# A two-block network: GpSimd's subtractions in eight operations a stage, and the written order of the steps replaced

## What is computed

```python
def first_block(x, ...):
    for l in range(DEPTH):                                   # DEPTH = 2
        proj = _rms(x, norm_g[l]) @ w_in[l]
        (gq, gk, gv, ga, gz, bq, bk, bv, iq, ik, iw, bz,
         cq, ck, cv, cz, gate) = jnp.split(proj, SPLIT_AT, axis=-1)
        y_a = _gla(gq, gk, gv, ga, ...) * silu(gz)           # linear attention with decay
        y_b = _dsa(bq, bk, bv, iq, ik, iw, ...) * silu(bz)   # an index picks 128 keys of each query
        y_c = _diff(cq, ck, cv, ...) * silu(cz)              # (softmax 1 - lam * softmax 2) V, 4 heads
        g = sigmoid(gate.reshape(B, T, 3, D_MODEL))
        x = x + (g[:, :, 0] * (y_a @ w_br[l, 0]) + g[:, :, 1] * (y_b @ w_br[l, 1])
                 + g[:, :, 2] * (y_c @ w_br[l, 2])) @ w_out[l]

def hybrid_layer(x, mod, ...):                               # second block, DEPTH layers
    h = rms_norm(x, norm1) * (1.0 + scale1) + shift1
    u, q, kv, gates = split(h @ w_in)
    mix = concatenate([pool_mixer(u), nsa_mixer(q, k, v, gates)]) @ w_out
    x = x + gate1 * mix
    h2 = rms_norm(x, norm2) * (1.0 + scale2) + shift2
    x = x + gate2 * (square(relu(h2 @ w_ff1)) @ w_ff2)       # 1024 to 4096 to 1024
```

## Time and profile before

| | |
|---|---|
| time before, median of 3 runs | 2624.44 us (2624.35 to 2630.99) |
| the profiled execution | 2632.11 us |
| its span, first to last instruction | 2630.3 us |
| TensorE busy, of the span | 2462.2 us, 94% |
| VectorE, ScalarE, GpSimd busy | 1337.0, 953.0 and 942.5 us |
| mean granted clock of TensorE | 0.975 |

### The profile page before, as it was taken

How to read it: one execution, slowest core, us unless ns; L and a number is a source line. 1 busy time by engine, 2 the same in 40 slices (tenths; PEclk the granted TensorE clock), 3 DMA queues, 4 the chain that set the end, 5 groups by cost and what they waited for, 6 DMA issues and landing times.

```text
span 2630.3 us, 34432 instructions
## 1 busy us (share of the span) xinstructions
PE 2462.2 (94%) x12303; PEld 1972.6 (75%) x12303; DVE 1337.0 (51%) x2835; ACT 953.0 (36%) x1691; POOL 942.5 (36%) x728
## 2 busy tenths in 40 slices
PE   7999989989999898998988898999998889899999
PEld 6687878678868686867887557888888656788887
DVE  4587243544368724354466545444566644522325
ACT  4442243432443224343244543322224444332221
POOL 4243414244434341423433103554544201344442
PEclk9999999999999999999999999999999989999999
DMA  5232414135423241413432102444433201233332
GB/s 174 72 97 90 151 35 142 50 103 177 135 71 96 87 161 33 137 49 112 171 99 61 33 3 71 160 161 150 163 118 99 69 1 33 65 97 96 96 96 81
DMA packets 132177, 256.04 MB, mean 97 GB/s; under 512 B 21915, under 2 KB 28589, under 8 KB 132013
## 3 DMA queue, kind: packets, MB, share of 16 engines
q1 hardware_dynamic: 132012, 253.83, 30.7%
HBM read 249.60 MB, written 4.19 MB: 96 GB/s over the span
## 4 chain that ended last, share of the span: by engine, by line
PE 79%; DVE 14%; ACT 4%; issue 2%; DMA 0%; DVEq 0%; SPq 0%; ACTq 0%
PE ps L818 65%; PE ps L772 4%; PE ps L1069 1%; PE ps L965 1%; PE ps L1118 1%; DVE arena L1768 1%; DVE top L1766 1%; PE ps L880 1%; PE ps L945 1%; ACT arena L1431 1%; PE ps L940 1%; DVE ps L1706 1%; DVE nsm L1477 1%; DVE ps L1704 1%; PE ps L1056 0%
## 5 line engine op out<-in xcount | busy, mean ns | idle before, releaser
L749 POOL TENSOR_TENSOR wl<-raw,wh 128x512 fp32r<-128x512 f32 (+2 forms) x724 | 942.3, 1326 | 1660.1 <-ACT wh L1139 1659.5
L818 PE MATMUL ps<-wh,hTh 128*128 128x512 f32 (+3 forms) x1600 | 633.6, 396 | 4.0 <-POOL wl L749 3.0
L818 PE MATMUL ps<-wh,hTl 128*128 128x512 f32 (+3 forms) x1600 | 614.7, 384 | 0.0
L818 PE MATMUL ps<-wl,hTh 128*128 128x512 f32 (+3 forms) x1600 | 614.5, 384 | 0.0
L1139 ACT ACTIVATE wh<-raw 128x1024 fp32r<-128x1024 f32 (+2 forms) x362 | 378.1, 1048 | 515.2 <-PE ps L818 269.9
L818 PEld LDWEIGHTS ps<-wh,hTh 128*128 128x128 f32 x1600 | 303.6, 190 | 77.8 <-issue 17.9
L818 PEld LDWEIGHTS ps<-wh,hTl 128*128 128x128 f32 x1600 | 303.1, 189 | 58.0
L818 PEld LDWEIGHTS ps<-wl,hTh 128*128 128x128 f32 x1600 | 304.0, 190 | 50.3
L818 PE MATMUL ps<-hTh,wh 128*128 128x512 f32 (+2 forms) x704 | 259.5, 369 | 5.6 <-DVE hTl L1710 2.3
L818 PE MATMUL ps<-hTl,wh 128*128 128x512 f32 (+2 forms) x704 | 258.2, 367 | 0.0
L818 PE MATMUL ps<-hTh,wl 128*128 128x512 f32 (+2 forms) x704 | 258.1, 367 | 0.0
(11 more groups left out here) (274 smaller groups left out, 3186.3 us busy)
## 6 DMA issues: line engine op xcount, KB each, us to landing
raw<-in_w_in_dram SPq DMA_DIRECT2D x160, 512.0 KB, 3.6
raw<-in_w_ff_dram SPq DMA_DIRECT2D x128, 512.0 KB, 3.6
modw<-in_w_mod_dram SPq DMA_DIRECT2D x96, 512.0 KB, 4.7
raw<-in_w_br_dram SPq DMA_DIRECT2D x24, 512.0 KB, 3.7
raw<-in_w_out_dram SPq DMA_DIRECT2D x24, 512.0 KB, 3.6
xm<-in_x_dram SPq DMA_DIRECT2D x8, 512.0 KB, 4.3
...
```

The source lines that it names most:

```text
L749: last = pool.tensor_tensor(low[part], whole[part], high[part], ALU.subtract)
L818: last = pe.matmul(*args, start=(q == 0 and c == 0 and n_pass == 0), stop=(q == u["quarters"] - 1 and c == u["chunks"] - 1 and n_pass == 2))
```

## The change

1. **GpSimd.** A stage's subtraction is made in eight operations in place of two: `128x128` each for a stage of 512 columns, 96 or 102 columns for the narrower ones. TensorE still waits for the last of a stage, where the semaphore is raised.
2. **The order.** `FIRST`, `SECOND` and `MOVED` are written anew. The work is the same but for the split of more sweeps in halves: the timeline has 2244 steps where it had 2222, with as many matmuls for each.
3. **A wait.** `rstd.bq` no longer stands between `small_turn` and the first `index` step, so the VectorE part of the first `index` step of a layer waits for ScalarE's part of `small_turn` itself.

That the roots of block two lie in the memory of the sums (PSUM) is so in both kernels; the code for it is not in the diff. The lines of the changed kernel that are named below stand 8 or 10 lower than before (749 is 757, 1893 is 1903).

The diff, with a few lines of each table:

```diff
@@ FIRST
-iq.0.0 q_turn.b.2 q_turn.b.3 iq.0.1 iq.0.2 iq.0.3 iq.1.0 iq.1.1 iq.1.2 iq.1.3 small.0.0 small_turn rstd.bq
+iq.0.0 q_turn.b.2 q_turn.b.3 iq.0.1 iq.0.2 iq.0.3 iq.1.0 rstd.bq iq.1.1 iq.1.2 iq.1.3 small.0.0 small_turn
...
@@ MOVED (of each engine's pairs those that the text speaks of)
-MOVED = {"act": """prob_turn.b.0.0>logit_exp.b.0.2 cq.1.1>prob_turn.b.1.1 decay3.2>decay3.3 mix0.0.2>mix0.0.1
+MOVED = {"act": """prob_turn.b.0.0>logit_exp.b.0.2 pair_exp.2.0.0>pool_band.1 pair_exp.1.1.2>pool_band.1 logit_exp.c.3.3>gate11.1.1
+                   k_rope.0>ek.1.2 pool.3>pair_turn.3.0.2 logit_exp.c.1.3>y_tok.c.0 ev.0.2>ev.0.1 bk.0.2>index.1.5
...
+                   prob.c.3.3>logit_max.c.3.3 prob.c.1.1>logit_max.c.1.1 y_tok.b.0>logit_max.b.2.0 evac.cz.1>logit_max.c.0.0
...
@@ -740,7 +748,7 @@
                 low, whole, high = piece(wl, g % RING, u), piece(raw, g % RING, u), piece(wh, g % SPLIT, u).bitcast(F32)
-                n = u["chunks"] * u["n"] // 2
+                n = u["chunks"] * u["n"] // 8
                 width = u["n"] if n >= u["n"] else n
@@ -1746,6 +1754,8 @@
                     W = WIDTH[t]
+                    if t == 0 and h == 0:
+                        dve.wait_ge(act_result, at("small_turned", l))
                     dve.wait_ge(act_result, at("relu", step))
```

More of the change, by code:

```diff
@@ L123 @@
-prob_turn.b.2.2 logits.b.3.1 logit_max.b.3.0 logit_exp.b.3.0 prob.b.2.3 value.b.2.0 prob_turn.b.2.3
-logit_exp.b.3.1 logits.b.3.2 logit_max.b.3.1 prob.b.3.0 value.b.2.1 logit_max.b.3.2 y_turn.b.1 ck.0.1
-prob_turn.b.3.0 logits.b.3.3 logit_exp.b.3.2 prob.b.3.1 value.b.2.2 ck.0.2 prob_turn.b.3.1 logit_max.b.3.3
-prob.b.3.2 logit_exp.b.3.3 value.b.2.3 y_tok.b.2 prob_turn.b.3.2 prob.b.3.3 value.b.3.0 ck.0.3 prob_turn.b.3.3
-value.b.3.1 y_turn.b.2 ck.1.0 value.b.3.2 value.b.3.3 rstd.cq y_tok.b.3 ck.1.1 ck.1.2 y_turn.b.3 ck.1.3 rstd.ck
@@ new lines @@
+prob_turn.b.0.2 value.b.0.0 logits.b.1.0 logits.b.1.1 logit_max.b.1.0 logit_exp.b.1.0 prob.b.0.3 cq.0.3
+logits.b.1.2 prob_turn.b.0.3 cq.1.0 logit_max.b.1.1 logit_exp.b.1.1 prob.b.1.0 value.b.0.1 prob_turn.b.1.0
+logits.b.1.3 logit_max.b.1.2 prob.b.1.1 q_turn.c.0 value.b.0.2 logit_exp.b.1.2 q_turn.c.1 prob_turn.b.1.1
+logits.b.2.0 logit_max.b.1.3 logit_max.b.2.0 value.b.0.3 prob.b.1.2 logit_exp.b.1.3 y_tok.b.0 cq.1.1
+prob_turn.b.1.2 logits.b.2.1 logit_exp.b.2.0 prob.b.1.3 value.b.1.0 prob_turn.b.1.3 logits.b.2.2 logit_max.b.2.1
@@ new lines @@
+logit_exp.b.2.1 prob.b.2.0 y_turn.b.0 cq.1.2 logit_max.b.2.2 prob_turn.b.2.0 logits.b.2.3 value.b.1.1
+logit_exp.b.2.2 prob.b.2.1 value.b.1.2 cq.1.3 prob_turn.b.2.1 logits.b.3.0 logit_max.b.2.3 logit_exp.b.2.3
+prob.b.2.2 value.b.1.3 y_tok.b.1 ck.0.0 q_turn.c.2 q_turn.c.3 logits.b.3.1 logit_max.b.3.0 logit_exp.b.3.0
+prob.b.2.3 prob_turn.b.2.2 value.b.2.0 prob_turn.b.2.3 logit_exp.b.3.1 logits.b.3.2 logit_max.b.3.1 value.b.2.1
+y_turn.b.1 ck.0.1 prob.b.3.0 logit_max.b.3.2 logits.b.3.3 prob.b.3.1 prob_turn.b.3.0 prob.b.3.2 value.b.2.2
@@ new lines @@
+logit_exp.b.3.2 ck.0.2 logit_max.b.3.3 prob_turn.b.3.1 logit_exp.b.3.3 value.b.2.3 prob_turn.b.3.2 prob.b.3.3
+ck.0.3 prob_turn.b.3.3 value.b.3.0 value.b.3.1 y_turn.b.2 ck.1.0 value.b.3.2 value.b.3.3 y_tok.b.2 rstd.cq
+y_tok.b.3 ck.1.1 ck.1.2 y_turn.b.3 ck.1.3 rstd.ck cv.0.0/ cv.0.0 cv.0.1 cv.0.2 cv.0.3 key_turn.ck.0
+key_turn.ck.1 cv.1.0 key_turn.ck.2 cv.1.1 cv.1.2 cv.1.3 cz.0.0 cz.0.1/ cz.0.1 cz.0.2 cz.0.3 cz.1.0 cz.1.1 cz.1.2
+key_turn.ck.3 cz.1.3 gate10.0.0 logits.c.0.0 logit_max.c.0.0 logit_exp.c.0.0 gate10.0.1 logit_max.c.0.1
@@ new lines @@
+prob.c.1.2 logit_max.c.1.3 logit_exp.c.1.3 value.c.0.3 y_tok.c.0 br10.0.1 prob_turn.c.1.2 logits.c.2.0
+logit_max.c.2.0 value.c.1.0 logit_exp.c.2.0 br10.1.0 prob_turn.c.1.3 prob.c.1.3 prob.c.2.0 logits.c.2.1
+logit_max.c.2.1 logit_exp.c.2.1 value.c.1.1 br10.1.1 prob_turn.c.2.0 logits.c.2.2 prob.c.2.1 logit_exp.c.2.2
+value.c.1.2 gate11.0.0 prob_turn.c.2.1 logits.c.2.3 logit_max.c.2.2 prob.c.2.2 logit_max.c.2.3 logit_exp.c.2.3
+value.c.1.3 y_tok.c.1 prob.c.2.3 gate11.0.1 prob_turn.c.2.2 logits.c.3.0 logit_exp.c.3.0 logit_max.c.3.0
@@ new lines @@
+value.c.2.0 gate11.0.2 gate11.0.3 prob.c.3.0 prob_turn.c.2.3 logits.c.3.1 logit_exp.c.3.1 value.c.2.1 gate11.1.0
+prob_turn.c.3.0 logits.c.3.2 logit_max.c.3.1 prob.c.3.1 logit_max.c.3.2 logit_exp.c.3.2 logit_exp.c.3.3
+value.c.2.2 gate11.1.1 prob.c.3.2 prob_turn.c.3.1 prob.c.3.3 logits.c.3.3 value.c.2.3 logit_max.c.3.3 y_tok.c.2
+gate11.1.2 prob_turn.c.3.2 value.c.3.0 gate11.1.3 prob_turn.c.3.3 value.c.3.1 br11.0.0 value.c.3.2 br11.0.1
+y_tok.c.3 value.c.3.3 br11.1.0 br11.1.1 y_turn.c.0 gate20.0.0 y_turn.c.1 gate20.0.1 y_turn.c.2 gate20.0.2
```

142 lines of the change are left out of this document (64 added, 78 removed).

## The result

The changed kernel takes 2616.84 us (median of 17 runs, 2606.16 to 2628.02), and the one before, on the same chips, 2631.88 (17 runs, 2621.71 to 2636.55). The ratio is 0.9948, 95% interval 0.9937 to 0.9958: 13.7 us less. The forecast was 31 less: the direction was right, and less than half of the size came.

What follows compares the result with a forecast made beforehand. TensorE bounds it, busy 2462.2 of 2630.3 us, so only idle time and lost clock can be won. Terms sum to 41.0, less costs 38, four fifths kept 31: 2624.4 - 31 = 2593 us, range 2574 to 2618.

Steps and rivals of the forecast that it cites:

- rstd.bq: First index step: root taken during the iq sweeps, so waits of 2.5 us and 1.4 of clock go; 3.9 us.
- the same, on VectorE: VectorE's operations beside GpSimd's shorter subtractions: each loses less, 2.5 us gained in all, between 0 and 8.
- The prediction's own signs: Signs named ahead: VectorE's small operations not above 0.7 us; wrong if TensorE's idle time falls under 15 us or over 50.
- GpSimd held up by VectorE: Rival: subtractions wait for VectorE's running operations, up to 6.7 us a stage; 12 us more, 2605; chance 0.07.
- GpSimd itself: GpSimd's eight operations: 0.44 us each at 128 columns, 3.5 a stage, mostly hidden; +0.7 a layer at ev.0.3.
- prob.c.3.3: Put ahead of y_tok.c.2 on VectorE: TensorE's wait of 5.46 us goes and its clock stays up; 15.8 in two layers.
- Block 1's order: Order terms 15.8, 2.4, 2.2, 3.9 and 7.0 us, from earlier prob steps, the root and attention b.
- the fifth that was cut off: Allowance on the sum: waits that go often leave the next late, so four fifths of 38 us kept, 31.
- Block 2: Waits of k_rope and q_rope steps shrink with more work ahead: 3.6 us a layer, 7.2, between 2 and 12.
- y_tok.c.0: Its chain on VectorE begins earlier by two exponentials, shortening TensorE's 4.75 us wait by 1.2; 2.4 in two layers.
- c.3.1: Maximum of 1024 columns no longer stands between, so the wait for ScalarE's L1346 goes; 2.2 us.
- Attention b: Matmuls of cq.1.0 cover prob_turn.b.1.0's 2.10 us wait, other waits shrink: 3.5 a layer, 7.0, between 4 and 11.

Runs made afterwards that it cites:

- mending this one wait: Changed kernel with two subtractions a stage for bv and gqk only, the stages beside topk's masks; ratio to the kernel before 0.9918.
- the burst of 512 columns: Kernel without the network: GpSimd runs 6 subtractions of 512 columns, VectorE comes in early; small operations took up to 1.19 us.
- the measurement of 12 to 22 us: Kernel without the network, VectorE let in late into bursts of 24 or 48 subtractions; holds such as 13.26 us at 128 columns, 22.80 at 256.
- block 1's table alone: Kernel before with block 1's new table and moves, block 2's old ones, two subtractions a stage; ratio 0.9881, 31 us less.

## Why the prediction was wrong

**The step that failed** is "the same, on VectorE": "a single operation that meets a subtraction loses at most 0.44 in place of up to 1.1", hence a gain of 2.5 us "between 0 (chains alone) and 8". Both ends had the sign of a gain. What the runs showed: a single operation lost up to 8.7 us in the changed kernel, and the mask 7.4, which made TensorE wait 15.0 us for `decay1` in two layers. Eight operations cost 14 us against two in the new order (0.9948 against 0.9894), and mending this one wait gave 8 back. For operations that come early in a run of subtractions the step was right, to the hundredth (0.38 to 0.44). It took for a law what the earlier trace rows show for the first to fourth subtraction of a run, that one operation gets through at each boundary. Nothing in the trace of before spoke against it: its longest run without a break is 8 operations. With eight a stage two stages make 16. The small gain that the step promised may be there: in the old order eight operations have 4.2 us less idle time than two. But the kernel was 6 us slower, with 10.5 us more busy time at a lower clock, and why the clock fell stays open. I worked out what becomes longer and shorter by the count of operations, and never asked what might depend on the count itself. The prediction's own signs show it: VectorE's small operations were to stay under 0.7 us, and one of two columns (L1671) took 2.92; TensorE's idle time fell by 13.8 us, under the 15 that it had named.

**The masks** were nowhere in the text. The place where a hold hurts most is where VectorE is the engine that has no rest: `topk` fills it for some 60 us with `decay1` right behind, which TensorE waited for by up to 1.8 us already. A term for that slack would have shown that little of 7.4 us more on this chain could be hidden. The profile shows them twice, with some 2 us of clock behind each: 4.61 us of work at a clock of 0.50 would be 2.3 at full clock, an estimate.

**The rival on this point had the wrong engine.** "GpSimd held up by VectorE" was priced at 12 us. GpSimd is held up, a subtraction by up to 1 us (at most 1499 ns, median 462), but TensorE waits only 1.9 us in two for it. The sentence of the Trainium skill, SBUF — State Buffer, "Who interferes with whom", that whoever issues first gets the pair for its whole instruction, speaks of one instruction. By that rule the burst of 512 columns agrees (1.19 us, one subtraction); late in a run the measurement of 12 to 22 us decides, and it is not one instruction's time.

**GpSimd itself** came out as worked out: 0.44 us and 3.5 a stage against 0.46 and, pair by pair, 13.48 / 4 = 3.4; busy 1280 against "1250 to 1350"; no stage late but at `ev.0.3`, 1.9 us in all. The line through two widths held at a third of its lowest width.

**`prob.c.3.3`**: 15.8 forecast, 16.0 measured alone. In the trace the wait of 5.46 us is gone and the clock is 1.00; TensorE's wait for L1835 behind it grew a little, from 0.66 us to 1.02.

**Block 1's order** was 31.3 of the sum (15.8, 2.4, 2.2, 3.9, 7.0), and block 1's table alone gave 31. So the fifth that was cut off it for waits that move was not needed. **Block 2** was 7.2 and gave -3 with two operations, within the intervals nothing, though TensorE's idle time fell by 5.9; the size, "twice what the two rows carry", had no ground. That the new order alone gave 28, near the 31 forecast for everything, is in part luck: the cut stood against a block 2 that did not show in the time.

**`y_tok.c.0`**: 1.2 forecast, and the wait went from 4.75 to 3.7. **`c.3.1`**: 2.2 forecast; the wait for L1354 is 3.8 us in four in the changed kernel, where it was 3.0, and 0.8 in two with two operations. **`rstd.bq`**: of 2.5 us of waits 0.8 was saved, since a later one at L1767 is 1.7 in two; the clock in the stretch from 79 to 84 us is 1.00 where it was 0.66. **Attention b**: 7.0 forecast; the wait for L1887 (5.0 us in four) is gone and the one for L1284 fell from 6.2 to 4.2.
